# Hybrid decoder trunk: the recurrent half's norm is applied behind the output projection, the last tile's values follow the second's, and small spreads and rotations read more rows

## What is computed

```python
att = mla_mixer(cq, ckv, kr, cos, sin, ...)
rnn = rglru_mixer(xr, gt, ...)            # h_scan * gelu(gate)
mix = jnp.concatenate([rmsnorm(att, attn_out_g[l]), rmsnorm(rnn, rnn_out_g[l])], axis=-1)
h = h + mix @ w_out[l]
u = rmsnorm(h, norm_ffn_g[l])
```

## Time and profile before

| | |
|---|---|
| median of 3 runs | 995.0 us (993.83 to 995.2) |
| profiled execution | 994.27 us, of which the span of instructions is 992.5 |
| PE busy | 943.3 us (95%), 5804 matmuls |
| DVE busy | 723.4 us (73%) |
| ACT busy | 576.4 us (58%) |
| mean granted TensorE clock | 0.968 |

### The profile page before, as it was taken

One profiled execution on the slowest core, in us unless ns is written; L12 is line 12 of the kernel. 1 busy time (PEld: TensorE's weight loads), 2 busy tenths in 40 slices (PEclk: granted clock), 3 DMA queues, 4 the chain that ended last, 5 costly groups with the idle time before them and its releaser, 6 DMA issues.

```text
span 992.5 us, 15412 instructions
## 1 busy us (share of the span) xinstructions
PE 943.3 (95%) x5804; PEld 839.4 (85%) x5804; DVE 723.4 (73%) x944; ACT 576.4 (58%) x796; POOL 42.3 (4%) x78
## 2 busy tenths in 40 slices
PE   5999989999999999999988899999999999999995
PEld 4974768999999999864767798989899989999993
DVE  5665775666666555656665688979897999899993
ACT  5465464545544344454453687676767777777771
POOL 4240000000000000000002000000000000000000
PEclk9999888999999999999879899999999999999997
DMA  9503111555559653414015189989998999899971
GB/s 273 176 1 126 46 43 47 172 168 175 183 179 243 174 171 102 127 43 128 1 64 191 54 311 353 328 300 350 349 339 289 365 339 348 289 345 351 341 284 45
DMA packets 120024, 203.84 MB, mean 205 GB/s; under 512 B 5874, under 2 KB 73740, under 8 KB 119964
## 3 DMA queue, kind: packets, MB, share of 16 engines
q1 hardware_dynamic: 119504, 202.81, 59.4%
q10 hardware_dynamic: 460, 0.23, 0.1%
HBM read 201.98 MB, written 1.05 MB: 205 GB/s over the span
## 4 chain that ended last, share of the span: by engine, by line
PE 85%; DVE 9%; ACT 3%; issue 1%; DMA 0%; ACTq 0%; DVEq 0%
PE ps L2294 22%; PE ps L2319 11%; PE ps L605 11%; PE ps L607 11%; PE ps L606 11%; DVE wlo L1302 4%; PE ps L1949 2%; PE ps L1873 2%; PE ps L2252 2%; PE ps L1879 2%; PE ps L1980 2%; PE ps L1998 1%; PE ps L1884 1%; ACT whi L883 1%; PE ps L2069 1%
## 5 line engine op out<-in xcount | busy, mean ns | idle before, releaser
L1302 DVE TENSOR_TENSOR wlo<-raw,whi 128x1536 fp32r<-128x1536 f32 (+4 forms) x296 | 437.4, 1506 | 90.2 <-ACT whi L883 88.1
L883 ACT ACTIVATE whi<-raw 128x1536 fp32r<-128x1536 f32 (+4 forms) x296 | 376.3, 1284 | 171.7 <-PE ps L607 90.9
L605 PE MATMUL ps<-uhi,whi 128*128 128x272 f32 (+1 forms) x576 | 171.1, 297 | 2.9 <-DVE ulo L1320 2.9
L607 PE MATMUL ps<-uhi,wlo 128*128 128x272 f32 (+1 forms) x576 | 168.9, 293 | 0.0
L606 PE MATMUL ps<-ulo,whi 128*128 128x272 f32 (+1 forms) x576 | 168.5, 292 | 0.0
L2294 PE MATMUL ps<-whi,xeh 128*128 128x320 f32 (+1 forms) x512 | 125.5, 326 | 0.0
L2294 PE MATMUL ps<-whi,xel 128*128 128x320 f32 (+1 forms) x512 | 124.2, 324 | 0.0
L2294 PE MATMUL ps<-wlo,xeh 128*128 128x320 f32 (+1 forms) x512 | 124.2, 324 | 0.0
L605 PEld LDWEIGHTS ps<-uhi,whi 128*128 128x128 f32 (+1 forms) x576 | 111.0, 193 | 7.7 <-issue 7.1
L606 PEld LDWEIGHTS ps<-ulo,whi 128*128 128x128 f32 (+1 forms) x576 | 111.3, 193 | 0.1
L607 PEld LDWEIGHTS ps<-uhi,wlo 128*128 128x128 f32 (+1 forms) x576 | 110.9, 193 | 0.0
(11 more groups left out here) (296 smaller groups left out, 1328.9 us busy)
## 6 DMA issues: line engine op xcount, KB each, us to landing
raw<-in_moe_w_down_dram SPq DMA_DIRECT2D x24, 1536.0 KB, 7.0
raw<-in_moe_w_gate_dram SPq DMA_DIRECT2D x16, 1536.0 KB, 7.5
raw<-in_moe_w_up_dram SPq DMA_DIRECT2D x16, 1536.0 KB, 8.2
raw<-in_moe_w_gate_dram SPq DMA_DIRECT2D x16, 1280.0 KB, 7.1
raw<-in_moe_w_up_dram SPq DMA_DIRECT2D x16, 1280.0 KB, 6.0
raw<-in_ffn_w_gate_dram SPq DMA_DIRECT2D x11, 1024.0 KB, 5.3
raw<-in_ffn_w_up_dram SPq DMA_DIRECT2D x11, 1024.0 KB, 5.3
raw<-in_ffn_w_down_dram SPq DMA_DIRECT2D x8, 1408.0 KB, 7.0
```

What stands on the lines that cost most here:

```text
L605: pe.matmul(dst, wh, xh, start=start, stop=False, skip_group_check=True)
L607: return pe.matmul(dst, wl, xh, start=False, stop=stop, skip_group_check=True)
L883: act.activation(placed(whi, s, src), src, ACT.Copy).then_inc(hi_done, 1)
L1302: dve.tensor_tensor(placed(wlo, s, src), src, placed(whi, s, src).bitcast(F32), ALU.subtract).then_inc(lo_done, 1)
```

## The change

The recurrent half is no longer normalized before `w_out`. With r its root mean square per token, it goes in as `xc` times its gain, and the attention half is multiplied by r as well (`rnd`, in `normed`); DVE multiplies each finished `w_out` block by 1/r on its way out of PSUM (`rr`), in an operation of its own, and then adds. r is computed per token on partitions: one-column matmuls (`variance`, in the last tile's values before item 6), a small DVE operation per use and two on GpSimd; `scale_spread` brings 1/r to all partitions with one matmul per tile. `values(2)` stands directly behind `values(1)`. `out_turned` of the other tiles moves behind the first recurrent half block of `w_out`, that of the last tile behind the second. ACT no longer loads the Sqrt table there, but before the second norm of layer 0. The low and high halves of `w_out` chunks 2 to 4, the first tile's average and the copies of the last tile take new places. `spread` reads all 128 rows (the stationary column picks the row), and the rotations of queries read 96.

New are `rnv`, `rnr`, `rnd` (128x3, `rnv` set to 1 at the start, as `rr` is) and the semaphore `rn_power`; `rn_root`, `rn_done` and `rg_done` go. The rest, in the order of the file:

```diff
 ATTENTION = [[("gt", 1), ("scores", 0), ("scores", 1), ("gt", 2), ("meta", 0), ("gt", 3), ("values", 0), ("scores", 2),
-              ("values", 1), ("rnss", None), ("values", 2), ("out", 0), ("out", 1), ("out", 2)],
-             [("gt", 1), ("scores", 1), ("gt", 2), ("gt", 3), ("scores", 2), ("values", 1), ("rnss", None),
-              ("values", 2), ("out", 1), ("out", 2)]]
+              ("values", 1), ("values", 2)],
+             [("gt", 1), ("scores", 1), ("gt", 2), ("gt", 3), ("scores", 2), ("values", 1), ("values", 2)]]
+OUT_BANK = (7, 4, 5)
+VAR_AT = 6
...
                 if t:
-                    for h in items(t):
+                    for i, h in enumerate(items(t)):
+                        if t == 2 and i == VAR_AT:
+                            add("rnvar", bank=3)
...
                 add("o", t, bank=5 - t % 2)
-            elif what == "out":
-                add("ot", t, bank=4 if t else None)
-            else:
-                add(what)
+        for t in tiles(l):
+            if t == 2:
+                add("rnbc", bank=6)
+            add("ot", t, bank=OUT_BANK[t])
...
                 average_power(1)
+                b = B[l, "rnvar"]
+                pool.wait_ge(emptied[b.bank], b.before + 1)
+                pool.tensor_tensor(rnr[:, :], rnv[:, :], mhalf[:, :].to_broadcast([P, 3]), ALU.pow).then_inc(rn_power, 1)
+                pool.wait_ge(rn_power, 2 * l + 1)
+                pool.tensor_tensor(rnd[:, :], rnv[:, :], rnr[:, :], ALU.mult).then_inc(rn_power, 1)
...
-                def rn_high():
-                    for c in range(CH):
-                        act.wait_ge(rg_done, CH * l + c + 1)
-                        act.activation(rnh[:, c, c0:T], tb[:, c, c0:T], ACT.Copy).then_inc(mixhi, 1)
+                def rn_high(c):
+                    act.wait_ge(rnn_done, CH * l + c + 1)
+                    act.activation(rnh[:, c, c0:T], xc[:, c, c0:T], ACT.Copy, scale=col("rnn_out_g", l, c)).then_inc(mixhi, 1)
...
                 gate_square(3)
+                mix(l, N_IN + 3)
+                if l == 0:
+                    out_squares(0)
...
                 for c in range(CH):
-                    rnn_square(c)
-                if l == 0:
-                    out_squares(0)
+                    rn_high(c)
+                rnn_square(0)
+                rnn_square(1)
+                turned(2, 1)
+                rnn_square(2)
+                rnn_square(3)
+                turned(2, 3)
                 out_squares(1)
-                root_all(B[l, "rnss"], rr[:, :], DH2, rn_root)
-                for h in range(1, NH, 2):
-                    turned(2, h)
-                    if h == 3:
-                        mix(l, N_IN + 3)
-                rn_high()
+                turned(2, 5)
+                turned(2, 7)
...
                 for t in tl:
+                    if t == 2:
+                        take(B[l, "rnbc"], rr[:, c0:T], cols=slice(c0, T))
...
                 if l == 0:
+                    mark(ACT.Sqrt)
...
                     dve.wait_ge(rstd_done, POWERS[l, ("att", t)])
-                    dve.tensor_scalar(osb_of(t), osb_of(t), rv[0:n, t:t + 1], None, ALU.mult)\
+                    dve.wait_ge(rn_power, 2 * (l + 1))
+                    dve.tensor_scalar(osb_of(t), osb_of(t), rv[0:n, t:t + 1], rnd[0:n, t:t + 1], ALU.mult, ALU.mult)\
...
-                def rn_scaled(cs):
-                    dve.wait_ge(rn_done, l + 1)
+                def rn_low(*cs):
                     for c in cs:
-                        dve.scalar_tensor_tensor(tb[:, c, c0:T], xc[:, c, c0:T], col("rnn_out_g", l, c),
-                                                 rr[:, c0:T], ALU.mult, ALU.mult).then_inc(rg_done, 1)
...
-                def rn_low():
-                    for c in range(CH):
                         dve.wait_ge(mixhi, high["rn"] - CH + c + 1)
-                        q = dve.tensor_tensor(rnl[:, c, c0:T], tb[:, c, c0:T], rnh[:, c, c0:T].bitcast(F32), ALU.subtract)
-                    q.then_inc(rnlo, 1)
+                        q = dve.scalar_tensor_tensor(rnl[:, c, c0:T], xc[:, c, c0:T], col("rnn_out_g", l, c),
+                                                     rnh[:, c, c0:T].bitcast(F32), ALU.mult, ALU.subtract)
+                    if CH - 1 in cs:
+                        q.then_inc(rnlo, 1)
...
+                def rn_variance():
+                    b = B[l, "rnvar"]
+                    dve.wait_ge(filled, b.ready())
+                    if l == 0:
+                        dve.tensor_scalar(rnv[0:NMETA, 0:1], ps[0:NMETA, b.bank, 0:1], 1.0 / DH2, EPS, ALU.mult, ALU.add)
+                    dve.tensor_scalar(rnv[:, 1:3], ps[:, b.bank, 1:3], 1.0 / DH2, EPS, ALU.mult, ALU.add)\
+                       .then_inc(emptied[b.bank], 1)
...
                     turned(0, META)
+                mix(l, N_IN + 1)
                 gelu_gate(3)
+                if l == 0:
+                    averages(0)
...
                 gelu_times(3)
-                if l == 0:
-                    averages(0)
...
                 turned(2, 0)
-                mix(l, N_IN + 1)
-                dve.wait_ge(rn_root, l + 1)
-                dve.reciprocal(rr[:, :], rr[:, :]).then_inc(rn_done, 1)
+                rn_low(0, 1)
                 turned(2, 2)
-                rn_scaled((0, 1))
+                rn_low(2, 3)
+                turned(2, 4)
+                rn_variance()
+                turned(2, 6)
+                turned(2, META)
...
                     normed(0)
-                turned(2, 4)
-                rn_scaled((2, 3))
                 normed(1)
-                turned(2, 6)
-                rn_low()
-                turned(2, META)
+                mix(l, N_IN + 2)
...
                 out_low(1)
-                mix(l, N_IN + 2, N_IN + 3)
                 normed(2)
+                mix(l, N_IN + 3)
...
+                b = B[l, "rnbc"]
+                dve.wait_ge(emptied[b.bank], b.before + 1)
...
                     dve.wait_ge(filled, b.ready())
-                    dve.tensor_tensor(hT[:, m, c0:T], hT[:, m, c0:T], bank(b, cols=slice(c0, T)), ALU.add)\
+                    dve.tensor_tensor(rsb[:, c0:T], bank(b, cols=slice(c0, T)), rr[:, c0:T], ALU.mult)\
...
                     dve.wait_ge(emptied[b.bank], b.before + 1)
-                    dve.engine_nop().then_inc(h_done, 1)
+                    dve.tensor_tensor(hT[:, m, c0:T], hT[:, m, c0:T], rsb[:, c0:T], ALU.add).then_inc(h_done, 1)
+                    dve.wait_ge(h_done, KD * (2 * l + 1) + m + 1)
...
-            def spread(bk, row, rows, width=P):
...
-                return pe.matmul(ps[0:width, bk, 0:T], ident[0:rows, row:row + 1].to_broadcast([rows, width]), rr[0:rows, :],
+            def spread(bk, row, width=P):
...
+                return pe.matmul(ps[0:width, bk, 0:T], ident[:, row:row + 1].to_broadcast([P, width]), rr[:, :],
...
                             fill(pe, b)
-                            spread(b.bank, row, 2).then_inc(filled, 1)
+                            spread(b.bank, row).then_inc(filled, 1)
...
                 r = slice(NOPE, QKH)
-                rot = con[r, C_ROT:C_ROT + ROPE]
+                rot, rot_all = con[r, C_ROT:C_ROT + ROPE], con[0:QKH, C_ROT:C_ROT + ROPE]
...
                     pe.wait_ge(emptied[u.bank], u.before + 1)
-                    pe.matmul(bank(b, r), rot, qT[r, h, :], start=True, stop=True).then_inc(filled, 1)
+                    pe.matmul(bank(b, r), rot_all, qT[0:QKH, h, :], start=True, stop=True).then_inc(filled, 1)
...
                     fill(pe, b)
-                    spread(b.bank, NH + h, 2 * NH, QKH).then_inc(filled, 1)
+                    spread(b.bank, NH + h, QKH).then_inc(filled, 1)
...
+                def variance():
+                    b = B[l, "rnvar"]
+                    fill(pe, b)
+                    pe.wait_ge(squares, (2 + CH) * (l + 1))
+                    for t in tiles(l):
+                        lead, n = TILES[t]
+                        for c in range(CH):
+                            q = pe.matmul(ps[0:n, b.bank, t:t + 1], ta[:, c, lead:lead + n], one[:, :], start=(c == 0),
+                                          stop=(c == CH - 1))
+                    q.then_inc(filled, 1)
...
                     for i in range(0 if p_too else 1, len(its) + (1 if o_too else 0)):
+                        if t == 2 and i == VAR_AT:
+                            variance()
...
                         values(t, p_too=t > 0)
-                    elif what == "out":
-                        out_turned(t)
-                    elif what == "rnss":
-                        b = B[l, "rnss"]
-                        fill(pe, b)
-                        pe.wait_ge(squares, (2 + CH) * (l + 1))
-                        total(b.bank, ta, CH).then_inc(filled, 1)
...
+                def scale_spread():
+                    b = B[l, "rnbc"]
+                    fill(pe, b)
+                    pe.wait_ge(rn_power, 2 * (l + 1))
```

(23 more changed lines are left out.)

## The result

The changed kernel takes 978.44 us (median of 4 runs, 975.04 to 980.14) against 994.42 (4 runs, 993.83 to 995.2): ratio 0.9834, 95% interval 0.9813 to 0.9855. The prediction was 988.5, range 980.0 to 993.5: the sign was right, the size 10 us short and outside the range. It is the fastest of the four (mean granted clock 0.980, the others 0.974 to 0.977), so what follows accounts for 19.2 us where the medians lie 16.0 apart.

A forecast was written before the change was run, and what follows sets the result against it. TensorE's chain of waits, 85% its own, was taken as the bound, with its clock halved around attention. Layer 0's -4.1 and layer 1's -2.0 gave -6.1 against the profiled 994.27: 988.2, put at 988.5 for the median, range 980 to 993.5.

The forecast's parts named there:

- Spreads of the latent scales: Latent-scale spreads, 2 to 128 rows: clock stays up, -1.0 us in layer 0, 0 in layer 1.
- Head-scale spreads: Head-scale spreads, 16 to 128 rows: full clock there and in the gt block, -2.75 us layer 0, -3.3 layer 1.
- rival 2: Both spreads: the clock does not hang on rows and still falls, 995.2 us; chance 0.12.
- Order before the last tile's exponentials: DVE's low half of the second w_out chunk ahead of gelu_gate(3), maxima(2): +0.15 us layer 0, +0.85 layer 1.
- Last tile directly behind the second's: Last tile's values, sum of squares replaced by variance matmuls: no gain at low clock, +0.25 us layer 0, +0.9 layer 1.
- rival 1: Values: the clock also comes back there, about -6 us a layer; one layer 982, both 976; chance 0.20.
- From averages(2) to the attention half: Stretch from averages(2) to w_out's attention half, low halves moved away: -0.75 us layer 0, -0.9 layer 1.
- Eviction of w_out: One more DVE operation per w_out block, hidden except the last in layer 1: +0.45 us.
- rival 4: w_out eviction: DVE's added work is uncovered, up to 7 us on top, 995; chance 0.04.
- rival 3: Variance before the last tile's remaining heads: 40 one-column instructions at 0.40 us each, slower than before, 997.8 us; chance 0.05.

The follow-up runs named there:

- rows_only: Kernel before with only the wide reads (spreads over 128 rows, rotations over 96, rr set to 1 at the start): 988.75 us, ratio 0.9925.
- after_nopad: Changed kernel with its three 128x3 tensors declared last in the mixers' memory, so all else lies as before: 985.57 us, ratio 0.9888.
- order_only: Changed kernel with the narrow spreads and rotations of before: 987.75 us, ratio 0.9919.
- before_pad: Kernel before with three unused 128x3 SBUF tensors behind mhalf, a shift of 36 bytes a partition: 991.72 us, ratio 0.9957.
- before_pad64: Kernel before with one unused tensor of 64 bytes a partition behind mhalf: 995.54 us, ratio 0.999.
- moe_pad: Kernel before with the three unused 128x3 tensors at the head of the experts' own memory only: 990.59 us, ratio 0.9945.
- rows_pad_gap: Kernel before with the wide reads, the three tensors and discarded matmuls in the second tile's waits, old order kept: 982.28 us, ratio 0.9853.
- lo_moved: Changed kernel with DVE's low half of the second w_out chunk moved from ahead of gelu_gate(3) to behind gelu_times(3): 977.5 us, ratio 0.9802.
- var64: Changed kernel with the variance matmuls' moving operand 64 columns wide instead of 1: 974.45 us, ratio 0.9779.
- gap_var64: Changed kernel with discarded matmuls in the second tile's waits and variance with 64 moving columns: 970.34 us, ratio 0.9734.

## Why the prediction was wrong, point by point

**Where the 19.2 us between the two profiles come from.** The executions reach the first latent spread at slightly different times (54.63 before, 54.39 in rows_only, 54.65 in after_nopad, 55.22 after), so I count to the first hidden matmul from there: 510.93, 504.79, 504.70 and 495.65. Rows 6.1; the order with the clock low 0.1; the clock's return in the last tile 9.05, which is what the two ways gain (4.22 + 4.86); addresses 4.55, in the experts' stage; 0.6 goes back for the later start. The prediction had 7.05 for the rows, +0.95 for the order, and neither of the other two in its sum.

- *Spreads of the latent scales, -1.0:* right. The queries follow the first of them at 59.96 - 55.22 = 4.74, against 60.37 - 54.63 = 5.74, held by DVE as worked out (its scaling ends at 59.86). In layer 1 there was no fall in the profile of before, and the step put 0; in four of the other five profiles with few rows (order_only, before_pad, before_pad64, moe_pad) there is one, at 421.9 to 424.2, and in none of the eleven with all rows.
- *Head-scale spreads, -2.75 and -3.3:* right. scores(0) comes 3.5 earlier with the latent part in it (3.75 forecast). From the first spread to scores(1) the changed kernel needs 471.82 - 463.48 = 8.34, against 482.61 - 471.03 = 11.58. In all eleven profiles with the wide reads that distance is 8.3 to 8.4 and the same in layer 0; in all six with few rows it is 11.0 to 12.4. The few rows were the cause; rival 2 is out. The rule behind it, that long idle gaps of PE let the clock fall (the Trainium skill, "TensorE: Matmul & The Clock Gate", "HAM oscillation — how this bites in real kernels"), does not cover this case: PE's idle 1.29 us ahead of the latent spreads is the same in both kernels and only the rows differ.
- *Order before the last tile's exponentials, +0.85:* right. In layer 1 maxima(2) starts 9.94 behind scores(1) (481.76 - 471.82), before 9.10 (491.71 - 482.61): 0.84. It was 0.2 in layer 0 against 0.15.
- *Last tile directly behind the second's, +0.25 and +0.9:* **this step failed.** It is the step in which "this edit by itself wins nothing while the clock is low" is taken as what will happen. Where the clock does stay low the size is fair: the way grows by 16.08 - 15.23 = 0.85 and 15.59 - 14.50 = 1.1 against 0.25 and 0.9, the variance with 3.74 and 3.38 being 0.3 and 0.4 over its 3.4 and 3.0. But in the changed kernel's profile it came back at the second tile's meta matmul in both layers, and the way is 11.86 and 10.73: rival 1, at 4.2 and 4.9 us a layer instead of 6 (the parts of its price add up to 6.8), to which I gave 0.20. That its 976 for both layers lies near the profiled 975.04 is luck: it had about 3 us too much for the clock and none of the 4.55 of the addresses. The argument against it was the packed stretch at 148 in the earlier trace rows that had not brought the clock back. It did not decide the case: packed values ran at the low clock through the whole way in after_nopad and at the full one from 136.00 to 142.90 here, so the stretch at 148, which began low, says nothing of values that begin with the clock up. What the prediction cited on transpositions does not tell the two apart either. That in the kernel before it was the stalls behind the sum that let the clock fall is my reading; rows_pad_gap fits it, no run tests it alone. Nor is the return a constant: order_only and lo_moved have one way with it and one without, and runs of after_nopad, order_only and var64 lie 7.6, 11.6 and 12 us apart.
- *From averages(2) to the attention half, -0.9 in layer 1:* the last meta matmul to that half is 512.55 - 502.31 = 10.24 against 527.74 - 516.31 = 11.43, -1.2 in the changed kernel; -0.96 in after_nopad. In layer 0 it is 157.76 - 145.87 = 11.89 against 165.39 - 152.87 = 12.52, -0.6 for the -0.75 forecast. Right.
- *Eviction of w_out, +0.45:* right. From the first attention matmul to the last router column it is 538.16 - 512.55 = 25.6, against 552.79 - 527.74 = 25.05, 0.56 more; the router's pairs stand 3.75 apart in both. Rival 4 is out.
- *Variance dear (rival 3):* out, with 0.09 to 0.21 us each.
- *Left out:* that three tensors of 12 bytes move everything allocated behind them. No step asked for it; 4.55 us, a quarter of the gain. The median lies 10 below the forecast: less the addresses, 5.5 are left for the clock, where the fastest execution had 9.05.

What stays open: why the clock comes back in one execution and not in the next of the same kernel, what makes the 32- and 36-byte placements cheaper (the loads of `heh` and `xeh`, or another engine's traffic to its own tensors), and why the 384-column matmuls gain more from 32 bytes than from 36. The experiments show the effects and not these mechanisms.

## What to carry to other kernels

Where TensorE's clock can be at either level, work out each step at both, and take the level itself as a case with a price; the removal of stalls is worth little at the low level and much more as soon as the clock can come back. Discarded matmuls in waits that exist anyway made that sure here and cost less than they gave; on the path itself they cost what they gave. A new tensor of a few bytes is a change of its own: time the kernel before with the same tensors added, or the gain will be put down to the wrong edit.

## What the runs showed that was not expected

- Matmuls of 512 and 384 columns in the experts' stage stand 5.7 and 2.9 ns closer when the stage's own tensors are shifted by 36 bytes a partition, and hardly with 64 bytes; 5.3 us over the stage, against 0.8.
- One-column matmuls are cheap (0.09 us each at the full clock and 0.156 at the low one where a third of them load 16 columns, 0.11 and 0.21 where all load 128), but at or behind 24 or 16 of them the clock fell in seven of eight ways; with 64 columns, for 0.3 us more (2.40 from the first of them to the next transposition, in gap_var64, against 2.09; 1.79 against 1.76 in layer 1), in none of five.
- One place in each layer at which the clock comes back or not goes with differences of 4 to 5 us each between ways of the same program; with the waits filled and the wide columns the runs of a kernel lie 2.5 us apart (968.6 to 971.07) instead of 12 (var64).
